# Norm sums in a hybrid decoder trunk: fp32 products replaced by two rounded products, with their low parts made on VectorE and GpSimd

## The reference

```python
def rms_norm(x, gain):
    xf = x.astype(jnp.float32)
    xf = xf * lax.rsqrt(jnp.mean(xf * xf, axis=-1, keepdims=True) + NORM_EPS)
    return (xf * gain.astype(jnp.float32)).astype(x.dtype)

for l in range(DEPTH):
    x = x + 0.5 * swiglu(rms_norm(x, ffn1_norm[l]), ffn1_w1[l], ffn1_w3[l], ffn1_w2[l])
    h = rms_norm(x, mix_norm[l])                   # mean over 1024 channels
    ...                                            # four branches of h, among them:
    # Mamba:     rms_norm(y * jax.nn.silu(z), norm_g)                       over 512 channels
    # attention: rope(rms_norm(q.reshape(b, L, 8, 64), q_norm), positions)  over the 64 of a head, k likewise
    x = x + merged @ w_out[l]
    x = x + 0.5 * swiglu(rms_norm(x, ffn2_norm[l]), ffn2_w1[l], ffn2_w3[l], ffn2_w2[l])
```

## Time and profile before

| | us |
|---|---|
| median of 3 runs | 2814.41 (2814.05 to 2815.18) |
| the profiled execution | 2814.93 |
| its span, first to last instruction | 2813.1 |

### The profile page before, as it was taken

One profiled execution on the slowest core, in us unless ns is written; L12 is line 12 of the kernel. 1 busy time (PEld: TensorE's weight loads), 2 busy tenths in 40 slices (PEclk: granted clock), 3 DMA queues, 4 the chain that ended last, 5 costly groups with the idle time before them and its releaser, 6 DMA issues.

```text
span 2813.1 us, 38529 instructions
## 1 busy us (share of the span) xinstructions
PE 2806.7 (100%) x14242; PEld 2294.4 (82%) x14242; DVE 1592.4 (57%) x2332; ACT 1177.3 (42%) x1699; POOL 706.1 (25%) x336
## 2 busy tenths in 40 slices
PE   9999999999999999999999999999999999999999
PEld 8888888777788888888888888888777888888888
DVE  5585557685557354343544855576846673543434
ACT  5342344655355344232443423445553653442322
POOL 0075023333333440000000840234333334400000
PEclk9999999999999999999999999999999999999999
DMA  5323573222223233333333335832222223333332
GB/s 197 97 91 128 140 164 99 83 69 76 81 76 90 90 98 92 100 96 95 96 127 97 94 125 141 157 98 86 72 75 78 86 82 90 93 99 98 94 97 90
DMA packets 113057, 284.11 MB, mean 101 GB/s; under 512 B 35616, under 2 KB 45344, under 8 KB 112416
## 3 DMA queue, kind: packets, MB, share of 16 engines
q1 hardware_dynamic: 112928, 282.35, 34.5%
HBM read 268.67 MB, written 9.44 MB: 99 GB/s over the span
## 4 chain that ended last, share of the span: by engine, by line
PE 97%; DVE 1%; DMA 1%; SPq 0%; ACT 0%; issue 0%; ACTq 0%; DVEq 0%
PE bank L499 29%; PE bank L501 28%; PE bank L500 28%; PE bank L527 1%; PE bank L529 1%; PE bank L528 1%; PE bank L812 1%; PE bank L831 1%; PE bank L846 1%; PE bank L592 1%; PE bank L945 1%; PE bank L786 0%; DMA s_ud<-s_uc 0%; PE bank L1003 0%; PE bank L720 0%; PE bank L1015 0%
## 5 line engine op out<-in xcount | busy, mean ns | idle before, releaser
L499 PE MATMUL bank<-h_hi,w_hi 128*128 128x512 f32 x2480 | 976.1, 394 | 0.6 <-DVE silu_a L1866 0.3
L501 PE MATMUL bank<-h_hi,w_lo 128*128 128x512 f32 x2480 | 965.6, 389 | 0.0
L500 PE MATMUL bank<-h_lo,w_hi 128*128 128x512 f32 x2480 | 965.4, 389 | 0.0
L426 ACT ACTIVATE w_hi<-raw 128x1024 fp32r<-128x1024 f32 x478 | 503.8, 1057 | 904.9 <-PE bank L501 879.9
L434 POOL TENSOR_TENSOR w_lo<-raw,w_hi 128x1024 fp32r<-128x1024 f32 x208 | 519.1, 2500 | 1084.7 <-ACT w_hi L426 1084.7
L499 PEld LDWEIGHTS bank<-h_hi,w_hi 128*128 128x128 f32 x2480 | 465.5, 188 | 105.3 <-issue 8.8
L501 PEld LDWEIGHTS bank<-h_hi,w_lo 128*128 128x128 f32 x2480 | 465.5, 188 | 97.8
L500 PEld LDWEIGHTS bank<-h_lo,w_hi 128*128 128x128 f32 x2480 | 465.8, 188 | 95.9 <-issue 1.7
L434 DVE TENSOR_TENSOR w_lo<-raw,w_hi 128x1024 fp32r<-128x1024 f32 x270 | 358.1, 1326 | 268.7 <-ACT w_hi L426 268.4
L499 PE MATMUL bank<-g_hi,w_hi 128*128 128x512 f32 x698 | 272.0, 390 | 0.0
L501 PE MATMUL bank<-g_hi,w_lo 128*128 128x512 f32 x698 | 271.6, 389 | 0.0
(11 more groups left out here) (375 smaller groups left out, 3346.9 us busy)
## 6 DMA issues: line engine op xcount, KB each, us to landing
raw<-in_w_lots SPq DMA_DIRECT2D x478, 512.0 KB, 3.6
s_wd<-s_z SPq DMA_DIRECT2D x8, 512.0 KB, 3.5
s_t<-s_taps SPq DMA_DIRECT2D x16, 256.0 KB, 13.4
da_s<-da_qk SPq DMA_DIRECT2D x16, 256.0 KB, 3.9
x<-in_x SPq DMA_DIRECT2D x8, 256.0 KB, 5.8
raw_k<-in_w_lots SPq DMA_DIRECT2D x8, 256.0 KB, 6.0
s_w_re<-s_wd SPq DMA_DIRECT2D x32, 64.0 KB, 3.8
s_w_im<-s_wd SPq DMA_DIRECT2D x32, 64.0 KB, 3.6
```

The costliest lines, as they stand in the source:

```text
L426: act.activation(w_hi[:, s], raw[:, s], AFT.Copy).then_inc(S["hi_done"], 1)
L499: pe.matmul(b[:, :], w_hi[:, s, kw], xh[:, k], start=(k == 0), stop=False)
L500: pe.matmul(b[:, :], w_hi[:, s, kw], xl[:, k], start=False, stop=False)
L501: return pe.matmul(b[:, :], w_lo[:, s, kw], xh[:, k], start=False, stop=(k == nk - 1))
```

## The change

The sums of squares over whole rows, over the Mamba channels and over the heads of queries and keys get one form: the fp32 sum or square is rounded to fp32r (high part, ScalarE, a Copy), the rest is the fp32 value less the high part, rounded as well (low part), and TensorE multiplies both with rounded ones and adds them up in the bank. The first row sum of the run (layer 0, r = 0) stays as it was.

- **Row sums**: `rstd_of` makes the high part before it waits for the sums, `low_sum` on VectorE the low part; both overlay `sq`. In `ffn` the products move behind the second gemm; in `quad` they stay.
- **Mamba norm**: the same with `m2_sh` and `m2_sl`, in the step `m2_square`.
- **Queries and keys**: a new step `da_high(g)`, four roundings on ScalarE and four subtractions on GpSimd (in place, over the squares). `da_high 0` stands behind the first half of `da_rope 0`, `da_high 1` behind `glu 1`, ahead of `da_index 3`. The key's high parts lie in the tiles of `da_s`, so ScalarE waits there for `da_rope` at 8.
- `blk_r` and `ones_r` are rounded copies of the two constant matrices, made once on VectorE (`blk_r` in each layer).

```diff
-    s += [..., ("s5_out", 1), ("da_square", 0), ("da_rope", 0, 0, 2), ("lot", "qi", 0), ("s5_back",)]
+    s += [..., ("s5_out", 1), ("da_square", 0), ("da_rope", 0, 0, 2), ("da_high", 0), ("lot", "qi", 0), ("s5_back",)]
...
-    s += [("da_index", 2), ("glu_mul", 0), ("da_rope", 1, 0, 4), ("glu", 1), ("da_index", 3)]
+    s += [("da_index", 2), ("glu_mul", 0), ("da_rope", 1, 0, 4), ("glu", 1), ("da_high", 1), ("da_index", 3)]
...
+        sum_hi = at("sum_hi", [P, SEQ], f32r, A + 28)
+        sum_lo = at("sum_lo", [P, SEQ], f32r, A + 29)
...
+        da_lo = [at("da_lo_q", [P, 4, SEQ], f32r, 0, extra), at("da_lo_k", [P, 4, SEQ], f32r, A + 8)]
+        da_hi = [[at("da_hi%d" % j, [P, SEQ], f32r, t) for j, t in enumerate((Y + 2, Y + 3, Y + 6, Y + 7))],
+                 [at("da_hi%d" % (4 + j), [P, SEQ], f32r, A + 4 + j) for j in range(4)]]
...
@@ TensorE, norm_sums
-                pe.wait_ge(S["sq_used"], KT * (R(r) + 1))
-                pe.matmul(bank[6][:, :], ones, sq_sum[:, :], start=True, stop=True).then_inc(S["sq_sums"], 1)
+                    pe.wait_ge(S["sq_used"], KT)
+                    pe.matmul(bank[6][:, :], ones, sq_sum[:, :], start=True, stop=True).then_inc(S["sq_sums"], 1)
+                    return
+                pe.wait_ge(S["sum_lo_done"], R(r))
+                pe.matmul(bank[6][:, :], ones_r[:, :], sum_hi[:, :], start=True, stop=False)
+                pe.matmul(bank[6][:, :], ones_r[:, :], sum_lo[:, :], start=False, stop=True).then_inc(S["sq_sums"], 1)
@@ TensorE, ffn
                             gemm(n, 0, h_hi, h_lo, KT, ready=("h_done", H(H_RAW[2 * which])))
+                            gemm(n + 1, 0, h_hi, h_lo, KT)
                             norm_sums(2 * which)
-                            for j in (1, 2, 3):
-                                gemm(n + j, 0, h_hi, h_lo, KT)
+                            gemm(n + 2, 0, h_hi, h_lo, KT)
+                            gemm(n + 3, 0, h_hi, h_lo, KT)
@@ TensorE, da_norm
-                    pe.wait_ge(S["da_sq"], 4 * g + j + 1)
-                    pe.matmul(bank[4 + j][:, :], C("blk"), da_t[g][:, j], start=True, stop=True).then_inc(S["da_ms"], 1)
+                    pe.wait_ge(S["da_low"], 4 * g + j + 1)
+                    pe.matmul(bank[4 + j][:, :], blk_r[:, :], da_hi[g][j][:, :], start=True, stop=False)
+                    pe.matmul(bank[4 + j][:, :], blk_r[:, :], da_lo[g][:, j], start=False, stop=True).then_inc(S["da_ms"], 1)
@@ TensorE, m2_norm
-                pe.wait_ge(S["m2_sum"], 3)
-                pe.matmul(bank[4][:, :], ones, m2_t[0][:, :], start=True, stop=True).then_inc(S["m2_ms"], 1)
+                pe.wait_ge(S["m2_sum"], 4)
+                pe.matmul(bank[4][:, :], ones_r[:, :], m2_sh[:, :], start=True, stop=False)
+                pe.matmul(bank[4][:, :], ones_r[:, :], m2_sl[:, :], start=False, stop=True).then_inc(S["m2_ms"], 1)
@@ GpSimd, mixing
+                    elif step[0] == "da_high":
+                        g = step[1]
+                        for j in range(4):
+                            pool.wait_ge(S["da_sq"], 8 * g + 4 + j + 1)
+                            pool.tensor_tensor(da_lo[g][:, j], da_t[g][:, j], da_hi[g][j][:, :].bitcast(f32), SUB) \
+                                .then_inc(S["da_low"], 1)
@@ ScalarE
             def rstd_of(r):
+                if R(r):
+                    act.wait_ge(S["sq_used"], KT * (R(r) + 1))
+                    act.activation(sum_hi[:, :], sq_sum[:, :], AFT.Copy).then_inc(S["sum_hi_done"], 1)
                 act.wait_ge(S["sq_sums"], R(r + 1))
...
+            def da_high_(g):
+                if g:
+                    act.wait_ge(S["da_rope"], 8)
+                for j in range(4):
+                    act.wait_ge(S["da_sq"], 8 * g + j + 1)
+                    act.activation(da_hi[g][j][:, :], da_t[g][:, j], AFT.Copy).then_inc(S["da_sq"], 1)
...
+                act.wait_ge(S["m2_sum"], 3)
+                act.activation(m2_sh[:, :], m2_t[0][:, :], AFT.Copy).then_inc(S["m2_sq"], 1)
@@ VectorE
+            def low_sum(r):
+                V.wait_ge(S["sum_hi_done"], R(r))
+                V.tensor_tensor(sum_lo[:, :], sq_sum[:, :], sum_hi[:, :].bitcast(f32), SUB).then_inc(S["sum_lo_done"], 1)
...
+                V.wait_ge(S["m2_sq"], BT + 1)
+                TT(m2_sl[:, :], m2_t[0][:, :], m2_sh[:, :].bitcast(f32), SUB).then_inc(S["m2_sum"], 1)
```

More of the change, by code:

```diff
@@ L81, in script @@
     s += [("lot", "q", 1), ("lot", "q", 2), ("s5_in",), ("lot", "q", 3), ("lot", "k", 0), ("s5_out", 0)]
-    s += [("lot", "k", 1), ("lot", "k", 2), ("s5_out", 1), ("da_square", 0), ("da_rope", 0, 0, 2), ("lot", "qi", 0), ("s5_back",)]
+    s += [("lot", "k", 1), ("lot", "k", 2), ("s5_out", 1), ("da_square", 0), ("da_rope", 0, 0, 2), ("da_high", 0), ("lot", "qi", 0), ("s5_back",)]
     s += [("s5_end",), ("lot", "qi", 1), ("da_rope", 0, 2, 4), ("lot", "k", 3), ("da_index", 1), ("da_square", 1), ("glu", 0)]
-    s += [("da_index", 2), ("glu_mul", 0), ("da_rope", 1, 0, 4), ("glu", 1), ("da_index", 3)]
+    s += [("da_index", 2), ("glu_mul", 0), ("da_rope", 1, 0, 4), ("glu", 1), ("da_high", 1), ("da_index", 3)]
     s += [("glu_end", 0), ("glu_mul", 1)]
@@ L271, in trunk @@
         extra = -(-(tail + 704 + 2 * TILE + 32) // 32) * 32
+        ones_r = at("ones_r", [P, P], f32r, 0, extra + 8 * TILE)
         s5_ca = at("s5_ca", [P, 2, 16, S5_Q + 1, 16], f32, A + 4)
@@ L330, in trunk @@
         m2_t = [at("m2_t%d" % i, [P, SEQ], f32, A + t) for i, t in enumerate((31, 32, 23, 24))]
+        m2_sh = at("m2_sh", [P, SEQ], f32r, A + 32)
+        m2_sl = at("m2_sl", [P, SEQ], f32r, A + 23)
         hq = at("hq", [P, 4, SEQ], f32, A)
@@ L366, in trunk @@
         ONCE = """act_seq dve_seq pool_seq mix_clear c_ones c_rest c_pos c_x0 c_x1 c_x2 c_x3 c_x4 c_x5 c_x6 c_x7 c_w0
-            p_hi p_lo p_step p_ang p_trig p_gam1 p_seq e_out""".split()
+            p_hi p_lo p_step p_ang p_trig p_seq e_out""".split()
         S = {}
@@ L769, in glu_end @@
                 pass
+            def da_high_(g):
+                pass
             def da_square(g):
@@ L1028, in _ @@
             STEPS = dict(lot=lot, pair=pair, turn_small=turn_small, out=out, out_start=out_start, glu=glu, glu_mul=glu_mul, glu_end=glu_end,
-                         gate=gate, branch=branch, merge=merge, da_square=da_square,
+                         gate=gate, branch=branch, merge=merge, da_square=da_square, da_high=da_high_,
                          quad=quad, s5_in=s5_in_, s5_out=s5_out, s5_back=s5_back,
@@ L1371, in trig @@
                    .then_inc(S["p_trig"], 1)
-                act.wait_ge(S["p_gam1"], 1)
+                act.wait_ge(S["p_ang"], 3)
                 act.activation(gtmp[:, 1], gtmp[:, 0], AFT.Exp).then_inc(S["p_trig"], 1)
@@ L1828, in normalise_h @@
             def normalise_h():
+                low_sum(1)
                 V.wait_ge(S["rstd_ready"], R(2))
@@ L1858, in ffn @@
                 n, g0 = nb, G(which)
+                if R(2 * which):
+                    low_sum(2 * which)
+                else:
+                    V.wait_ge(S["c_ones"], 16)
+                    V.tensor_copy(ones_r[:, :], ones)
                 V.wait_ge(S["rstd_ready"], R(2 * which + 1))
@@ L2070, in s5_in_ @@
                 chain(TT(pr[2], pr[2], cs, MUL))
+                do(V.tensor_copy(blk_r[:, :], C("blk")))
                 TT(s5_s[:, 1, :, 1:S5_CH + 1], rows(pr[0]), rows(pr[2]), ADD).then_inc(S["s5_state"], 1)
@@ L2110, in da_rope @@
                 for j in range(a, b):
-                    V.wait_ge(S["da_sq"], 4 * g + j + 1)
+                    V.wait_ge(S["da_sq"], 8 * g + j + 1)
                     qk = da_qk[:, 4 * g + j]
@@ L2433, in angles @@
                         pdo(ins)
-                ins.then_inc(S["p_gam1"], 1)
+                ins.then_inc(S["p_ang"], 1)
                 V.wait_ge(S["p_trig"], 3)
```

5 lines of the change are left out of this document (3 added, 2 removed).

## The result

The kernel after took 2830.36 us (median of 6 runs, 2829.51 to 2831.74), the one before 2814.12 (6 runs, 2814.03 to 2815.18): a ratio of 1.0057, 95% interval 1.0048 to 1.0067, so slower by 0.6%. The forecast was 2832.5, range 2816 to 2839. The profiled execution of after took 2831.74 with a span of 2830.0, 16.9 more than before's 2813.1.

The account below looks back on a forecast made before the run. TensorE was taken to bound the kernel, with 97% of the chain. Waits +21.1, da_norm 1 -3.2, row sums -2.0, Mamba -0.8 and clock +3.0 gave +18.1 on 2814.41: 2832.5 us, range 2816 to 2839.

Parts of the forecast that it names:

- Bound and gain per product: TensorE holds 97% of the chain; each of 23 replaced fp32 products gives 0.404 us, 9.3 in all.
- Covers in the row sums: Later low parts cause no TensorE wait: cover 0.8 in the quad, 4.5 in the FFN; gain 2.0.
- The Relu wait: Before da_norm 0, TensorE waits for Relus queued behind the key roundings: 3.0 in layer 0, 2.3 in layer 1.
- glu 2 later: Its gemm waits for the bank that glu_mul 1 frees: 10.9 later in layer 0, 10.2 in layer 1, sum 21.1.
- The shift of the rotation's end: VectorE's chain, delayed around GpSimd's query low parts, ends the key rotation 1.0 later, out of 0 to 1.6.
- R: End of VectorE's last key rotation, 492.72 in layer 0 before; glu_mul 1 was to end at R + 14.7.
- The clock: TensorE's stalls bring back about half rate: 0 to 2.8 per layer, 1.5 taken twice, 3.0 in all.
- The sum: Waits +21.1, da_norm 1 -3.2, row sums -2.0, Mamba -0.8, clock +3.0: +18.1, median 2832.5.
- 1: Rival: GpSimd gets only two key low parts between VectorE's steps; 2820, with clock up to 2823; chance 0.18, in-between included.
- 2: Rival: VectorE undisturbed by GpSimd, glu_mul 1 ends at R + 7.4; -1.4, so 2813.0; chance 0.08.
- 3: Rival: the wait costs nothing and the whole gain of 9.3 remains: 2805; chance 0.05.
- 4: Rival: lateness continues after glu 2 into da_norm 1 and attention, 2 to 4 more per layer: 2836 to 2841; chance 0.09.

Follow-up runs that it names:

- e1_rows: The kernel after with only row sums and Mamba norm in the new form, queries and keys as fp32 products: 2811.22 us, ratio 0.9989.
- e4_no_low: The kernel after without GpSimd's four key low parts, TensorE multiplying the key high parts twice instead: 2815.08 us, ratio 1.0002.
- e10_e6_later: e6_reordered with da_norm 0 moved behind glu 2 and glu_mul 2: 2807.11 us, ratio 0.9973.
- e6_reordered: The kernel after with glu_mul 1 ahead of the key rotation, da_high 1 behind glu_end 1, da_norm 1 behind glu 3: 2808.42 us, ratio 0.9978.
- e9_norm_later: e7_reordered2 with da_norm 0 moved behind glu 2 and glu_mul 2: 2807.44 us, ratio 0.9974.
- e7_reordered2: e6_reordered with glu_mul 0 also moved ahead of da_index 2: 2824.99 us, ratio 1.0036.
- e3_relus_first: The kernel after with da_high 1 moved behind da_index 3, so the key roundings follow its Relus: 2820.1 us, ratio 1.0017.

## Why the prediction was right, point by point

**Bound and gain per product: right.** Two rounded products take 0.47 (800.45 to 800.92 in the Mamba norm, layer 0, by the trace of after), four pairs of `da_norm 1` 1.87 (514.83 to 516.70) against 3.43. The products of the rows and the Mamba norm gave 3.3 (`e1_rows`) where 2.8 stood in the sum; their slots explain 2.7, and the rest is within the interval.

**Covers in the row sums: right.** In the quad the low part was ready at 374.43 and TensorE came at 375.23: 0.8, as worked out. In the FFN VectorE's first w_lo ended at 1075.35 and TensorE, which made the row sum at 1068.41, came to the fifth gemm at 1068.41 + 0.47 + 10.9 = 1079.8: 4.4 of cover.

**The Relu wait: right, a little too large.** 1.95 in each layer, against 3.0 and 2.3: the v pair itself ended later by 1.0 in layer 0, through the small waits before it.

**glu 2 later: the right mechanism, 4.0 too much.** In layer 0 glu 2 began at 506.51, 8.97 later, or 9.4 with the row sum's gain before it added back (10.9 foreseen); in layer 1 at 1916.24, 16.41 later, of which 8.65 was carried in, so 7.8 (10.2 foreseen). Sum 17.1 and not 21.1. Two terms were mis-sized. The shift of the rotation's end, taken as 1.0 each, was 0.7 and -0.2 (492.33 + 0.69 = 493.02 against 492.72, with the row sum's 0.4 added back; 1902.75 against 1894.29 + 8.65): in layer 0 VectorE was 1.0 late up to `glu_mul 0` (482.72 against 481.69), but its first rotation step then waited for the same GpSimd subtraction as before, whose time TensorE's lots set, and only 1.84 in place of 2.56: that turn swallowed most of the delay. And `glu_mul 1` ended at R + 13.3, not R + 14.7: the score steps began at R + 2.74 and not 2.9, and the turns cost 6.1 (0.3 on the first step, 1.8 on the next two, 2.0 each on the last and the mask), where 7.3 had been added. The handover took 0.15, which the sum did not have.

**The clock: right that it would fall, half its size.** 14 products took 6.03 (506.51 to 512.54) where 14 x 0.227 = 3.18 would do: 2.85, and the same in layer 1. 5.7 in all, 3.0 foreseen, and just over the 5.6 that was its upper bound. The bound came from the first products of the run, and it came near partly by luck: in those first microseconds of before the profile grants a clock of 1.00, so that they were slow for the same reason is not shown, while behind the stall in after it grants 0.50. The Trainium skill (TensorE: Matmul & The Clock Gate, Part 1), by which the clock falls when the engine has been idle and comes back only with sustained work, was the better guide here than the trace of before, which had no stall of this size to read it from. But not each stall paid: behind the first, of 1.95, six products still ran at 0.24, and the two slow ones after them lay inside the time for which TensorE then waited anyway.

**The sum.** 17.1 + 5.7 - 3.1 - 2.0 - 0.8 = 16.9, the difference of the spans. The two errors, -4.0 and +2.7, partly cancelled; a forecast within 2.1 of the result owes a part to that.

**Rivals.** 1 (no weight subtractions in the turns) fell: L2189 and L2192 show them. 2 (no disturbance) was the right price for a kernel without the low parts: R + 7.28 in `e4_no_low` against R + 7.4. 3 and 4 fell: TensorE had no new large wait behind glu 2.

## What to carry to other kernels

On a kernel whose TensorE never waits, price a change by what it does to the queues of the others: four roundings that waited for the rotation and their four subtractions on GpSimd cost twice what all the saved products gave, and the same work a few steps later left 7.5 of the 9.3 standing (`e10_e6_later`). Put the short step that frees a bank ahead of long chains that need nothing of it, and keep GpSimd's two-input work away from VectorE's chains, or behind the last step that TensorE waits for. A reordering that looks free by a few tenths can push one step into another engine's turn, so run it, and read what now stands behind the disturbed step.

## What the runs showed of the hardware

- VectorE and GpSimd take turns instruction by instruction, at every step with two SBUF tiles: GpSimd's 5.63 for four low parts and 5.19 for two weights ran almost at their own pace (5.01 and 2 x 2.4 elsewhere in the same trace), while VectorE's steps took 1.7 to 2.7 in place of 0.3 to 0.8. Steps with one tile and a bank were not held up: `glu_mul` 0.69 at 482.19 in `e6_reordered`, inside a GpSimd subtraction from 481.99 to 484.41, and 0.69 at 508.68 in `e9_norm_later`. Nor were the top-k steps (0.43) beside the key low parts. The Trainium skill (SBUF — State Buffer, SBUF: two separate sides) says that the shared ports are a lock held for a whole instruction, wanted by VectorE's operations with two SBUF inputs; these rows agree. A 128x128 mask that took 2.37 in place of 0.29 waited as long as a score step of 128x512 behind the same kind of subtraction (2.85 in place of 0.75, 496.27 in `e7_reordered2`): 2.1 each, so the price was set by GpSimd's instruction and not by the size of VectorE's own.
- A multiplication by a scalar with one tile as its input, L2185, was held up as well: 2.40 for 128x256 at 474.79 in `e6_reordered`, 0.15 behind the start of a GpSimd subtraction of 2.40, and 0.42 for 128x384 without one.
- Equal stalls have unequal prices. In `e4_no_low` the clock stayed up after a stall of 1.96 in layer 0, and after 1.94 in layer 1 all eight products ran at half rate. In after it fell behind the stall, while TensorE already worked again (slots of 0.24 until 498.77, then 0.39). After 4.1 in `e3_relus_first` the first 9 products took 3.72 in layer 0 and the first 13 took 5.66 in layer 1, where 0.227 each makes 2.04 and 2.95: 1.7 and 2.7 lost. A price for a stall of 2 to 4 is a range, here 0 to 2.7; after 6.7 to 6.9 it was 2.5 (layer 0 of `e7_reordered2`) and 2.85 (both layers of after).
